# Convolution stage: eight ACT products folded by two accumulating transfers of POOL, DVE with 17 taps

## What is computed

```python
u = jnp.einsum('bsd,de->bse', h, w1) + b1
a, gate = jnp.split(u, 2, axis=-1)
u = a * jax.nn.sigmoid(gate)
u = lax.conv_general_dilated(u, w_dw[:, None, :], window_strides=(1,),
        padding=[(CONV_WIDTH - 1, 0)], feature_group_count=D_MODEL) + b_dw   # width 31
u = jax.nn.silu(layernorm(u, ln_g, ln_b))
return jnp.einsum('bsd,de->bse', u, w2) + b2
```

## Time and profile before

| | us |
|---|---|
| median of 3 runs (896.63 to 896.92) | 896.91 |
| the profiled execution | 896.41 |
| its span, first to last instruction | 894.6 |
| PE busy in the span | 878.9 |
| DVE busy | 704.7 |
| ACT busy | 460.5 |
| POOL busy | 150.4 |

### The profile page before, as it was taken

How to read it: one execution, slowest core, us unless ns; L and a number is a source line. 1 busy time by engine, 2 the same in 40 slices (tenths; PEclk the granted TensorE clock), 3 DMA queues, 4 the chain that set the end, 5 groups by cost and what they waited for, 6 DMA issues and landing times.

```text
span 894.6 us, 11948 instructions
## 1 busy us (share of the span) xinstructions
PE 878.9 (98%) x4408; PEld 744.0 (83%) x4408; DVE 704.7 (79%) x948; ACT 460.5 (51%) x666; POOL 150.4 (17%) x127
## 2 busy tenths in 40 slices
PE   8999998999999999999999999999999999999996
PEld 8888876889888888888888889988888888888885
DVE  5899999867977769686868888797776968786856
ACT  5778686255372726344363644637272634436243
POOL 1599993380000020000000051000000000000000
PEclk9999999999999999999999999999999999999999
DMA  9614023305133131423314023123313142331202
GB/s 299 178 50 116 17 79 118 115 27 188 62 128 141 47 141 49 166 81 127 127 61 165 29 92 116 48 63 127 141 47 141 50 165 81 126 131 57 71 1 95
DMA packets 48376, 90.81 MB, mean 102 GB/s; under 512 B 1458, under 2 KB 18866, under 8 KB 48340
## 3 DMA queue, kind: packets, MB, share of 16 engines
q1 hardware_dynamic: 48340, 90.32, 29.1%
HBM read 88.22 MB, written 2.10 MB: 101 GB/s over the span
## 4 chain that ended last, share of the span: by engine, by line
PE 80%; POOL 8%; DVE 6%; DMA 2%; issue 2%; ACT 2%; SPq 0%; POOLq 0%; DVEq 0%; ACTq 0%
PE ps L1365 15%; PE ps L1366 15%; PE ps L1367 15%; PE ps L1599 10%; PE ps L1597 10%; PE ps L1598 10%; POOL w_lo L378 3%; POOL merged_a L388 3%; DMA w_raw<-in_conv_w 2%; POOL merged_b L388 2%; DVE ps L921 2%; PE ps L1384 1%; DVE tok L834 1%; PE ps L1511 1%; PE ps L1516 1%
## 5 line engine op out<-in xcount | busy, mean ns | idle before, releaser
L1365 PE MATMUL ps<-act_hi,w_hi 128*128 128x512 f32 (+1 forms) x704 | 259.8, 369 | 1.1 <-DVE act_lo L840 1.1
L1367 PE MATMUL ps<-act_hi,w_lo 128*128 128x512 f32 (+1 forms) x704 | 258.8, 368 | 0.0
L1366 PE MATMUL ps<-act_lo,w_hi 128*128 128x512 f32 (+1 forms) x704 | 258.8, 368 | 0.0
L1599 PE MATMUL ps<-w_hi,u_lo 128*128 128x512 f32 x392 | 152.7, 390 | 0.0
L1597 PE MATMUL ps<-w_hi,u_hi 128*128 128x512 f32 x392 | 152.7, 389 | 0.0
L1598 PE MATMUL ps<-w_lo,u_hi 128*128 128x512 f32 x392 | 152.5, 389 | 0.0
L1365 PEld LDWEIGHTS ps<-act_hi,w_hi 128*128 128x128 f32 x704 | 132.8, 189 | 23.2 <-DVE act_lo L840 1.4
L1367 PEld LDWEIGHTS ps<-act_hi,w_lo 128*128 128x128 f32 x704 | 132.8, 189 | 22.0
L1366 PEld LDWEIGHTS ps<-act_lo,w_hi 128*128 128x128 f32 x704 | 132.8, 189 | 21.7
L634 ACT ACTIVATE relu<-ps 128x512 f32<-128x512 f32 x36 | 21.5, 597 | 243.0 <-PE ps L1367 243.0
L1102 DVE TENSOR_TENSOR w_lo<-w_raw,w_hi 128x1024 fp32r<-128x1024 f32 x70 | 85.1, 1221 | 58.1 <-ACT w_hi L655 58.1
(11 more groups left out here) (219 smaller groups left out, 1299.1 us busy)
## 6 DMA issues: line engine op xcount, KB each, us to landing
w_raw<-in_mlp_w SPq DMA_DIRECT2D x32, 1024.0 KB, 4.8
w_raw<-in_mlp_w SPq DMA_DIRECT2D x16, 2048.0 KB, 8.0
w_raw<-in_conv_w SPq DMA_DIRECT2D x16, 512.0 KB, 5.6
w_raw<-in_conv_w SPq DMA_DIRECT2D x2, 2048.0 KB, 9.5
h<-in_x SPq DMA_DIRECT2D x4, 512.0 KB, 6.3
out<-tok SPq DMA_DIRECT2D x8, 256.0 KB, 2.2
gain<-in_norm_mix SPq DMA_DIRECT2D x2, 512.0 KB, 6.1
gain<-in_norm_mlp SPq DMA_DIRECT2D x2, 512.0 KB, 6.8
```

Source lines behind the costliest of these rows:

```text
L1365: nc.tensor.matmul(dst, lh, rh, start=(n == 0), stop=False)
L1366: nc.tensor.matmul(dst, lh, rl, start=False, stop=False)
L1367: return nc.tensor.matmul(dst, ll, rh, start=False, stop=(n == count - 1))
L1599: last = nc.tensor.matmul(dst, ll, rh, start=False, stop=(f == 1 and (closes or i not in (0, 5))))
```

## The change

In chunks 0 to 6 ACT makes eight products (`SHARE` 8) in `prod_a` and six for POOL (`POOL_SHARE` 6, five adds); DVE has 31 - 14 = 17 taps. POOL issues two transfers that add in flight (`accum_op`): slots 4 to 7 of the eight onto the first four (2048 elements, 8 KB a partition, 1 MB), then two of these onto the other two (0.5 MB). PE turns the merged sum, the two kept slots and DVE's sum, in `conv_turn`, after product e+2; `product_turn` is left for chunk 7 alone. The order in ACT's chunk is now: sigmoid, high part, copy, eight products, six for POOL; the fifth product waits until the first transfer of the chunk before has landed, because chunks share the slots 8 to 11. POOL waits for the eighth product and issues the first transfer ahead of its adds; after them it waits for the landing and issues the second. In chunk 7 the first product waits for chunk 6's first transfer, the seventh for its second.

```diff
-POOL_SHARE = 8
-SHARE = (5, 5, 5, 5, 5, 5, 5, 13)
+POOL_SHARE = 6
+SHARE = (8, 8, 8, 8, 8, 8, 8, 13)
+WIDE = 4
+KEPT = 2
+EARLY = 2 * WIDE
...
+        LAST_SLOT = (8, 9, 10, 11, 4, 5, 6, 7, 0, 1, 2, 3, 8)
+
+        def slot(e, n):
+            if e == NC - 1:
+                return LAST_SLOT[n]
+            return (e % 2) * WIDE + n if n < WIDE else WIDE + n
+
+        def ring(e, n):
+            return prod_a[:, slot(e, n), :]
+
+        def slots(e, n, count):
+            return prod_a[:, slot(e, n):slot(e, n) + count, :]
+
+        def folds(e):
+            return 16 * (e // 2 + 1)
...
                 into = merged[e % 2]
+                pool.wait_ge(prod_ok, FIRST[e] + EARLY)
+                nc.gpsimd.dma_start(slots(e, 0, WIDE), slots(e, WIDE, WIDE),
+                                    accum_op=ALU.add).then_inc(fold_one[e % 2], 16)
                 for t in range(1, POOL_SHARE):
...
+                pool.wait_ge(fold_one[e % 2], folds(e))
+                nc.gpsimd.dma_start(slots(e, 0, KEPT), slots(e, KEPT, KEPT),
+                                    accum_op=ALU.add).then_inc(fold_two[e % 2], 16)
...
+            def products(e):
 
                 act.wait_ge(glu_ok, e + 1)
-                if pooled_taps(e):
-                    pool_products(e, range(4))
...
+                for n in range(SHARE[e]):
+                    if e and n == WIDE:
+                        act.wait_ge(fold_one[(e - 1) % 2], folds(e - 1))
+                    product_of(e, n, POOL_SHARE + n)
+                    if n == EARLY - 1:
+                        pool_products(e, range(POOL_SHARE))
+
+            def last_products(which):
+
+                e = NC - 1
+                act.wait_ge(glu_ok, e + 1)
                 for n in which:
...
+                    if n == 0:
+                        act.wait_ge(fold_one[(e - 1) % 2], folds(e - 1))
+                    if n == 6:
+                        act.wait_ge(fold_two[(e - 1) % 2], folds(e - 1))
+                    if n == RING:
+                        act.wait_ge(prod_read, 1)
+                    product_of(e, n, n)
...
             def conv_turn(e):
-                if pooled_taps(e):
+                if e < NC - 1:
+                    if e >= 2:
+                        pe.wait_ge(ctok_ok, e - 1)
                     pe.wait_ge(padd_ok, (POOL_SHARE - 1) * (e + 1))
...
+                    turn_into(e, merged[e % 2], first=True)
+                    pe.wait_ge(fold_two[e % 2], folds(e))
+                    for n in range(KEPT):
+                        turn_into(e, ring(e, n))
                 pe.wait_ge(conv_ok, e + 1)
...
             for e in range(1, NC):
                 glu_product(e)
-                product_turn(e - 1, range(SHARE[e - 1]))
                 if e >= 2:
                     conv_turn(e - 2)
```

More of the change, by code:

```diff
@@ L183, in hybrid_encoder @@
         cwp_lo_ok, prod_ok, prod_read = sem("cwp_lo_ok"), sem("prod_ok"), sem("prod_read")
+        fold_one = [sem(f"fold_one{k}") for k in range(2)]
+        fold_two = [sem(f"fold_two{k}") for k in range(2)]
         conv_ok, conv_turned, ctok_ok = (sem(n) for n in ("conv_ok", "conv_turned", "ctok_ok"))
@@ L223, in hybrid_encoder @@
         LAST_TILES = (NQ - 1, 0)
-        def ring(k):
-            return prod_a[:, k % RING, :]
+        LAST_SLOT = (8, 9, 10, 11, 4, 5, 6, 7, 0, 1, 2, 3, 8)
[9 more added lines that the diff above has]
+            return 16 * (e // 2 + 1)
         def pool_ring(k):
@@ L516, in pool_products, with product_of @@
                                          scale=params[:, e, t:t + 1]).then_inc(pprod_ok, 1)
-            def products(e, which):
+            def product_of(e, n, t):
+                nc.scalar.activation(ring(e, n), upad[:, e % 2, t:t + S], ACT.Copy,
+                                     scale=params[:, e, t:t + 1]).then_inc(prod_ok, 1)
+            def products(e):
                 act.wait_ge(glu_ok, e + 1)
-                if pooled_taps(e):
-                    pool_products(e, range(4))
-                for n in which:
[L524 to L529, removed]
-                if pooled_taps(e):
-                    pool_products(e, range(4, POOL_SHARE))
+                for n in range(SHARE[e]):
[7 more added lines that the diff above has]
+                act.wait_ge(glu_ok, e + 1)
+                for n in which:
+                    if n == 0:
[5 more added lines that the diff above has]
+                    product_of(e, n, n)
             def c2_high(k):
@@ L551, in _ @@
                     ctok_copy(e - 2)
-                products(e, range(SHARE[e]))
+                products(e)
             gate(NC - 1)
@@ L557, in _ @@
             ctok_copy(NC - 3)
-            products(NC - 1, range(SHARE[NC - 1] // 2))
+            last_products(range(SHARE[NC - 1] // 2))
             c2_high(2)
             ctok_copy(NC - 2)
-            products(NC - 1, range(SHARE[NC - 1] // 2, SHARE[NC - 1]))
+            last_products(range(SHARE[NC - 1] // 2, SHARE[NC - 1]))
             c2_high(3)
@@ L1422, in glu_product, with turn_into @@
                 last.then_inc(glu_mm, 1)
[L1424 to L1434, removed]
+            def turn_into(e, src, first=False, last=False):
+                for b in range(NB):
+                    step = nc.tensor.matmul(ps[:, 4 + e % 2, block_cols(b)], src[:, block_cols(b)], ident[:],
+                                            is_transpose=True, start=(first and b == 0), stop=(last and b == NB - 1))
+                return step
@@ L1436, in conv_turn, with product_turn @@
+            def product_turn(which):
+                e = NC - 1
+                pe.wait_ge(ctok_ok, e - 1)
+                for n in which:
+                    pe.wait_ge(prod_ok, FIRST[e] + n + 1)
+                    turn_into(e, ring(e, n), first=(n == 0)).then_inc(prod_read, 1)
             def conv_turn(e):
-                if pooled_taps(e):
+                if e < NC - 1:
+                    if e >= 2:
+                        pe.wait_ge(ctok_ok, e - 1)
                     pe.wait_ge(padd_ok, (POOL_SHARE - 1) * (e + 1))
-                    for b in range(NB):
-                        nc.tensor.matmul(ps[:, 4 + e % 2, block_cols(b)], merged[e % 2][:, block_cols(b)], ident[:],
-                                         is_transpose=True, start=False, stop=False)
+                    turn_into(e, merged[e % 2], first=True)
+                    pe.wait_ge(fold_two[e % 2], folds(e))
+                    for n in range(KEPT):
+                        turn_into(e, ring(e, n))
@@ L1442, in conv_turn @@
                 pe.wait_ge(conv_ok, e + 1)
                 if e == NC - 1:
[L1444 to L1449, removed]
@@ L1450, in conv_turn @@
-                last.then_inc(conv_turned, 1)
+                    turn_into(e, relu[:, 1 - e % 2, :])
+                turn_into(e, relu[:, e % 2, :], last=True).then_inc(conv_turned, 1)
             def first_upper_half(cols):
@@ L1484, in _ @@
                 glu_product(e)
-                product_turn(e - 1, range(SHARE[e - 1]))
                 if e >= 2:
                     conv_turn(e - 2)
-            product_turn(NC - 1, range(SHARE[NC - 1] // 2))
+            product_turn(range(SHARE[NC - 1] // 2))
             conv_turn(NC - 2)
@@ L1491, in _ @@
                 pe.wait_ge(plast_ok, n + 1)
[L1492 to L1495, removed]
+                turn_into(NC - 1, prod_b[:, n, :])
+            product_turn(range(SHARE[NC - 1] // 2, SHARE[NC - 1]))
             conv_turn(NC - 1)
```

## The result

| | before | after |
|---|---|---|
| median, us | 896.77 | 908.55 |
| profiled execution, us | 896.41 | 908.57 |
| its span, us | 894.6 | 906.8 |
| start of the clock-keeping matmuls, us | 139.44 | 153.05 |

The changed kernel is slower: the ratio is 1.0127, interval 1.0113 to 1.0141. Three executions lie between 908.13 and 908.57; a fourth took 1468.74 us with a mean granted clock of 0.557 and is not in the ratio. The forecast was 904.4. The median of the kernel before is 896.77 here and 896.91 ahead of the prediction, because one more execution, 896.21, came in.

What follows compares the result with a forecast made beforehand. POOL carried over half the early chain, at 14.5 us a chunk, with PE 14.0 and DVE 13.4 close. Transfer waits moved the last turns from 139.44 to 146.9: 896.41 + 7.5 = 903.9, 904.4 us on the median's scale; range 889 to 920.

Steps and rivals of the forecast that it cites:

- F with a load: First transfer's time from issue to landing with a weight load beside it: 8.0 plus 2.5, so 10.5 us.
- x, what an issue holds POOL: Time that issuing a transfer holds POOL's queue, twice a chunk: taken as 1.0 us, with no row showing it.
- F without a load: First transfer's time from issue to landing with no load beside it: 8.0 us, by the 2 MB read.
- Second transfer: Landing time of the transfer half as big as the first: 4.8 us.
- The period: POOL's time for a chunk, including its wait for the first landing: 16.1 us with a load, 13.8 without.
- Chunk 5's transfer: First transfer of chunk 5, beside the 2 MB load: 10.5 us, landing at 125.5, with the last sigmoid at 131.7.
- From the last sigmoid to the end of the turns: ACT's casts, copies and products, a wait for chunk 6's transfer, then PE's turns: from 131.7 to 146.9 us.
- The clock: Rival, chance 0.06: PE at 1.2 GHz on reaching L1404's 24 matmuls, 5.5 us more, about 909, or 897 with transfers hidden.
- From there a shift is carried whole: From the clock-keeping matmuls at 139.44 us on, a shift reaches the kernel's end undiminished; the forecast shift was 7.5 us.
- The rival that the transfer hides: Chance 0.33: first transfer lands within 8.2 us even beside loads, POOL's chunk takes 13.8, kernel 891.9 us (890 to 894).
- The slow add: Rival, chance 0.14: first transfer takes 11.2 us alone, 13.7 with a load; POOL's chunk 19.3, kernel about 926 us.
- the blocked POOL: Rival, chance 0.03: the issue holds POOL until the transfer has landed; 24.6 us a chunk, over 60 us slower.

Runs made afterwards that it cites:

- As a copy: Changed kernel with both transfers copying instead of adding, which leaves products out of the sum: 889.79 us, ratio 0.992.
- with one transfer: Changed kernel without the second transfer; PE turns the four sums of the first instead of two: 898.81 us, ratio 1.0019.
- with sixteen slots: Changed kernel without the second transfer, PE turning four sums, and with 16 slots for ACT's products: 890.74 us, ratio 0.9937.
- the run made for it: Changed kernel with 14 and 20 matmuls that nobody reads ahead of PE's two last long waits: 907.73 us, ratio 1.0121.
- The run with all loads late: Changed kernel with SP's loads held until a chunk's first transfer landed, the 2 MB load until the last second transfer landed: 895.75 us, ratio 0.9987.
- the run with two transfers and all three helps: Changed kernel with 16 slots, the second issue behind the next chunk's subtraction, and all loads late: 895.23 us, ratio 0.9981.

## Why the prediction was right, point by point

The direction, the mechanism, the range (889 to 920) and the forecast's own range (899 to 913) held; the size fell short by 4.2 us. That F with a load came out right is partly luck, since two misses in it cancel. Against the working:

- **x, what an issue holds POOL** (1.0 taken). Held. The first issue is recorded with 1.13 us and overlaps the first add, which takes 1.85 instead of 1.40; from issue to that add's end it is 2.46, so some 1.0 to 1.1 for the issue. The second delays the subtraction's end by 66.00 + 4.81 - 65.39 - 4.65 = 0.8. As a copy an issue holds 0.6. The working calls 1.4 POOL's smallest step; the four products that it makes for chunk 7 take 2.71 us together, 0.68 each.
- **F without a load** (8.0). High by 1: 6.93 at 132.03, and 7.1 for chunk 4. The prediction's estimate by the Trainium skill (DMA: Bandwidth & Descriptors, Anatomy of one DMA), 6.8 for the 2 MB that are read, agrees with both. The working's sum by that estimate is wrong, though: 1.2 us less on each of four periods, on chunk 5's transfer and on chunk 6's makes 7.2, so +0.3 and not near +2.
- **F with a load** (10.5). Held: 11.09, 10.97, 9.87 and 10.79, on average 10.7. The share of the load was 3.7, not 2.5, and made up for the 1 above; that is the luck.
- **Second transfer** (4.8). Held, 4.5.
- **The period** (16.1 with a load, 13.8 without). Held: 16.3 on average, 13.2. Chunk 5's first issue came at 115.29, forecast 115.0. This includes 0.4 us by which POOL starts later in this execution (32.43 against 31.98). ACT's fifth product waited from chunk 1 on (2.16 us there, 4.84 in chunk 2), not from chunk 3.
- **Chunk 5's transfer** (10.5, the same as beside a 1 MB load). Mis-sized: beside the 2 MB load it took 13.60, +3.1. With that the last sigmoid comes at 135.06, forecast 131.7.
- **From the last sigmoid to the end of the turns** (15.2 forecast, 18.0 measured). Here a term was missing: the copy's wait for PE. The sum went from the sixth product over cast and copy straight to the last seven; but the copy needs chunk 6's sums, and PE turns these only behind the 24 turns of chunk 7's first six products, and the two kept ones only when the second transfer has landed (issued 139.77, landed near 144.3). Forecast 9.5 us from the sigmoid to the last seven products, measured 147.30 - 135.06 = 12.2, +2.7. The landing is the smaller part: with one transfer the same copy still waits 3.20 us (PE partly at half clock), and 2.43 with sixteen slots. PE's order of turns alone keeps the copy to about 10.3 us behind the sigmoid (4.9 to the first turn, 3.5 for 24 turns, 1.75 for 16 more, 0.2 to the copy; an estimate from these rows, where the forecast had 9.0); landing and half clock add the rest, to 11.8, of which the clock owns 0.8 by the run made for it. The kernel before had this wait too, with 0.68.
- **The clock** (0.06, worth 5.5). It did fall to 0.50, three times in this stage, but not where the rival had it: PE works from 139.92 on, and L1440's matmuls run at full clock again (5.70 us for 24, before 5.73). Worth 0.8 at the last chunk by the run made for it.
- **"From there a shift is carried whole"** (13.6 measured at the clock-keeping matmuls). It is not: 12.2 of it reach the end. Sum of the misses on the profiled executions: 0.3 for the start, 3.1 for chunk 5's transfer, 2.7 for the copy's wait and -1.4 here make 4.7, on the 7.5 forecast gives the 12.2 measured.
- **DVE** (12.76 a chunk when free). Its first chunks begin (`upad`) at 30.45, 43.20 and 55.96 us: 12.76 apart. After that it waits for ACT, as forecast.
- **The rival that the transfer hides** (891.9). Its 136.6 for the end of the turns doesn't follow from its sigmoid at 120.0: with the forecast's own 15.2 behind it, it is 135.2. The run with all loads late is that case, F 8.0: its pace is (102.82 - 32.70)/5 = 14.0, forecast 13.8. It gave 895.75, since the missing term is in it too (ACT waits 3.3 at 133.46).
- **The slow add** fell (F alone is 7), and so did the blocked POOL (adds start 0.6 us behind the issue).

The cause is shown in this sense: loads moved out of the transfers' way give back 12.8 us, more than the 11.8 lost; each wait removed alone gives back 0.8 to 5.3, because the next of them stands right behind; taking the second transfer away gives back 9.7. Not shown is where on the way of the bytes loads and transfers get into each other's way; that they do is shown.

## What to carry to other kernels

An accumulating transfer took twice the DMA time of a copy of the same bytes, and it meets first the load that the same event triggers: draw both on one time line before costing it. Put no engine's queue behind its landing (here POOL's subtraction, ACT's ring, PE's sums); with slots enough and one transfer, landings of 8.8 to 11 us cost nothing. When an edit takes the waits away, look again for the engine that sets the pace: a queue that runs ahead of it (here POOL at 12.45 us while PE takes 13.53) shows the wrong period. In a sum, follow each PSUM bank to its last addend and through the queue of the engine that adds it, not only the engine that is named as late.

## What the runs showed of the hardware that was not expected

- Copies landed in 5.8 and 3.2 us where adds took 10.8 and 4.5 in the median, beside the same loads, and their issues held POOL for 0.58 us instead of 0.85 to 1.14.
- The slowing is mutual: 512 KB loads went from 5.6 to 7.6 us in the median, and a 2 MB load beside the 1 MB add took 14.9 us instead of 7.5, the add 13.6 instead of 6.9. Beside copies the 512 KB loads took 7.8, no less than beside adds.
- In the run with two transfers and all three helps PE's clock fell behind a wait of 2.34 us, and cost time there.
- A wait at the far end of the kernel vanished. Before, DVE waited 1.13 us for an output transfer just ahead of the last rows, as DVE's timeline of the kernel before shows:

```profile
887.60 0.69 DVE L1337 TENSOR_TENSOR tok<-h,gain 128x512 f32<-128x512 f32 x1 [1.13 <-DMA out<-tok]
```

The same operation in the changed kernel's timeline has no wait:

```profile
899.56 0.68 DVE L1373 TENSOR_TENSOR tok<-h,gain 128x512 f32<-128x512 f32 x1
```

That code is the same in both. It is 0.95 of the 1.4 us that the shift loses on its way; the other 0.45 is a shorter wait of PE for the normalised rows (0.37 instead of 0.82). In the changed kernel and in all ten of the experiments, the span moved by 1.40 to 1.46 us less than the clock-keeping matmuls. Why the output transfer lands earlier there stays open; it was not tried.
